# The first up quad of each layer as seven products, begun while T is made; a fifth weight slot

## What is computed

```
x = x + concat(out_a, out_b) @ w_out          # the out tiles
h = rmsnorm(x, g_ffn)
z = dwconv3_centred(h @ w_up)                 # w_up: 1024 x 5632, gate and value halves
x = x + (silu(z_gate) * z_val) @ w_down       # w_down: 2816 x 1024
```

## Time and profile before

| | us |
|---|---|
| runs | 1079.54, 1079.80, 1079.80 |
| median | 1079.80 |
| the profiled execution | 1079.64 |
| its span, first to last instruction | 1077.7 |
| TensorE busy | 1063.8 |
| GpSimd, VectorE, ScalarE busy | 701.4, 596.9, 585.3 |

### The profile page before, as it was taken

The page is one execution under the profiler, slowest core; times in us unless marked ns, Lnnn a source line. Parts: engine busy times, 40 slices in busy tenths (PEclk is TensorE's granted clock), DMA queues, the critical chain, the costliest instruction groups (busy, mean ns, idle before and its releaser), DMA issues.

```text
span 1077.7 us, 18823 instructions
## 1 busy us (share of the span) xinstructions
PE 1063.8 (99%) x6780; PEld 949.1 (88%) x6780; DVE 596.9 (55%) x906; ACT 585.3 (54%) x812; POOL 701.4 (65%) x374
## 2 busy tenths in 40 slices
PE   9999999999999999999999999999999999999997
PEld 7788888798899989998878888888979998899987
DVE  4735765856246730776636359466561776136664
ACT  8835435665366633775548344555653774257641
POOL 5333335896999857995534333558959995699940
PEclk9999999999999999999999999999999999999999
DMA  8332124676798757972522221427759976689502
GB/s 305 99 98 79 59 61 155 162 171 196 184 227 216 203 155 171 210 165 96 177 79 87 79 79 60 156 78 181 188 146 267 209 165 195 165 191 236 153 20 78
DMA packets 48048, 161.75 MB, mean 150 GB/s; under 512 B 5584, under 2 KB 8400, under 8 KB 47952
## 3 DMA queue, kind: packets, MB, share of 16 engines
q1 hardware_dynamic: 35728, 117.51, 34.0%
q0 software_dynamic: 11520, 41.95, 21.5%
q10 hardware_dynamic: 704, 1.07, 0.3%
HBM read 137.44 MB, written 2.10 MB: 129 GB/s over the span
## 4 chain that ended last, share of the span: by engine, by line
PE 84%; DVE 5%; issue 4%; ACT 3%; POOL 2%; DMA 1%; DVEq 0%; ACTq 0%; SPq 0%; POOLq 0%
PE acc L1926 12%; PE acc L1929 12%; PE acc L1928 12%; PE acc L1630 11%; PE acc L1631 11%; PE acc L1632 11%; PE acc L1757 3%; PE acc L1758 3%; PE acc L1759 3%; DVE arena L1482 1%; POOL w_lo L543 1%; DVE arena L1419 1%; PE sides L1727 1%; PE sides L1845 1%; PE sides L1829 1%
## 5 line engine op out<-in xcount | busy, mean ns | idle before, releaser
L543 POOL TENSOR_TENSOR w_lo<-w_raw,w_hi 128x1024 fp32r<-128x1024 f32 x108 | 276.2, 2661 | 84.1 <-ACT w_hi L940 68.2
L553 POOL TENSOR_TENSOR w_lo<-w_raw,w_hi 128x1024 fp32r<-128x1024 f32 x52 | 125.2, 2413 | 202.6 <-ACT w_hi L652 202.6
L1630 PE MATMUL acc<-feat_hi,w_hi 128*128 128x512 f32 (+1 forms) x496 | 190.2, 383 | 2.8 <-POOL w_lo L543 1.8
L1631 PE MATMUL acc<-feat_lo,w_hi 128*128 128x512 f32 (+1 forms) x496 | 189.7, 382 | 0.0
L1632 PE MATMUL acc<-feat_hi,w_lo 128*128 128x512 f32 (+1 forms) x496 | 189.6, 382 | 0.0
L1928 PE MATMUL acc<-xg_lo,w_hi 128*128 128x256 f32 x608 | 172.1, 283 | 0.0
L1929 PE MATMUL acc<-xg_hi,w_lo 128*128 128x256 f32 x608 | 172.1, 283 | 0.0
L1926 PE MATMUL acc<-xg_hi,w_hi 128*128 128x256 f32 x608 | 172.0, 283 | 0.0
L1926 PE MATMUL acc<-t_hi,w_hi 128*128 128x256 f32 x480 | 136.0, 283 | 1.2 <-ACT arena L1005 1.2
L1928 PE MATMUL acc<-t_lo,w_hi 128*128 128x256 f32 x480 | 135.8, 283 | 0.0
L1929 PE MATMUL acc<-t_hi,w_lo 128*128 128x256 f32 x480 | 135.8, 283 | 0.0
(11 more groups left out here) (187 smaller groups left out, 2269.2 us busy)
## 6 DMA issues: line engine op xcount, KB each, us to landing
w_raw<-slabs SPq DMA_DIRECT2D x142, 512.0 KB, 4.4
arena<-slabs SPq DMA_DIRECT2D x32, 512.0 KB, 4.4
mixer_sb<-slabs SPq DMA_DIRECT2D x26, 512.0 KB, 5.8
arena<-slabs POOLq DMA_DIRECT2D x20, 512.0 KB, 6.1
w_raw<-slabs POOLq DMA_DIRECT2D x20, 512.0 KB, 5.9
second_s<-slabs SPq DMA_DIRECT2D x10, 512.0 KB, 5.5
second_s<-arena POOLq DMA_DIRECT2D x10, 512.0 KB, 7.8
mixer_sb<-second_s POOLq DMA_DIRECT2D x10, 512.0 KB, 4.9
```

The source lines that it names most:

```text
L543: pool.tensor_tensor(w_lo[:, w], source, w_hi[:, w].bitcast(F32), ALU.subtract).then_inc(lo_done, count)
L553: pool.tensor_tensor(w_lo[:, w], w_raw[:, w], w_hi[:, w].bitcast(F32), ALU.subtract).then_inc(lo_done, 1)
L1630: pe.matmul(out, wh, ah, start=first, stop=False)
L1631: pe.matmul(out, wh, al, start=False, stop=False)
```

## The change

- The first quad becomes a product quad like the ten others, in an order of its own: A11, A12, S4 (which take tokens as they are), then S1, S2, A22, S3. Its units are 28 to 34.
- S4 of that quad needs A12's raw block again (`a12_again`) and is summed in slot 2's raw buffer (`first_s4`).
- T1 is made where it stays: in the block of the tokens' buffer (`xg12_hi`, `xg12_lo`) that is not used in this part. So `gain_hi` and `gain_lo` write only half of the even tiles, `t_high(k)` and `t_low(k)` each have one operation more (256 columns), and the move at the end of the part is gone.
- The room of T1 in feat2 is a fifth weight slot, for S4 of the last quad of the first part and for the fifth down tile. The first four down tiles then wait for units one product earlier (`unit_before`).
- The loads, sums and conversions of the first quad stand among the out tiles on SyncE, GpSimd and ScalarE.

The diff, cut to what matters for the order:

```diff
+FIRST_ORDER = (A11_, A12_, S4_, S1_, S2_, A22_, S3_)
+LAST_OF_FIRST = unit_of(FIRST_QUADS - 1, S4_)
+FIFTH_SLOT = (LAST_OF_FIRST, DOWN_UNIT[0] + RING)
+def unit_before(unit):
+    if unit == LAST_OF_FIRST:
+        return N_FFN - 1
+    if unit == DOWN_UNIT[0] + RING:
+        return LAST_OF_FIRST
+    if DOWN_UNIT[0] <= unit < DOWN_UNIT[0] + RING:
+        return unit - 2 * RING
+    return unit - (2 * RING if unit == DOWN_UNIT[0] + 2 * RING else RING)
...
 # ScalarE
                 def t_high(k):
+
+                    act.wait_ge(t1_raw_done, L * KP + (k + 1))
+                    act.activation(xg12_hi[:, k, :], t1_raw[:, k * H:(k + 1) * H], ACT.Copy).then_inc(t1_hi_done, 1)
                     act.wait_ge(t_raw_done, L * KP + (k + 1))
...
+                high_a11(0)
                 out_tile(4)
                 t_high(1)
+                high_a12(0)
                 out_tile(5)
                 scale_pair(2)
-                first_high(0)
                 out_tile(6)
-                first_high(1)
+                high_s4(0)
+                t_high(2)
                 out_tile(7)
-                t_high(2)
+                high_s1(0)
                 scale_pair(3)
-                first_high(2)
-                first_high(3)
+                copy(0, A11_, 1, u3_copy)
+                high_s2(0)
+                high_a22(0)
+                t_high(3)
                 root("ffn_spread", stdT_done, L * NSIDE + NSIDE, rstdT[:, :], 1.0 / D, S)
-                t_high(3)
-                act.activation(t1_hi, t1_raw, ACT.Copy).then_inc(t1_hi_done, 1)
-                first_quad()
+                high_s3(0)
+                high_s1(1)
+                copy(0, S1_, 3, p5_copy)
+                copy(0, S2_, 1, u2_copy)
+                high_a11(1)
+                high_a12(1)
+                copy(0, S3_, 1, p1_copy)
...
-                    if d == 0:
-                        for to, of in ((xg12_hi, t1_hi), (xg12_lo, t1_lo)):
-                            act.activation(to, of.rearrange("p (k s) -> p k s", k=KP), ACT.Copy).then_inc(t1_moved, 1)
...
 # VectorE
                 def t_low(k):
+                    t1 = t1_raw[:, k * H:(k + 1) * H]
+                    dve.wait_ge(t1_hi_done, L * KP + (k + 1))
+                    dve.tensor_tensor(xg12_lo[:, k, :], t1, xg12_hi[:, k, :].bitcast(F32),
+                                      ALU.subtract).then_inc(t1_ready, 1)
...
-                    if m in (3, 4):
-                        t_low(m - 3)
-                t_low(2)
+                    if m in (3, 4, 6):
+                        t_low(m // 2 - 1 if m > 3 else 0)
+                first_c11()
+                t_low(3)
                 token_scale(L * 2 + 1)
...
-                first_quad()
+                first_rest()
...
 # TensorE
+                def first_products():
...
+                    tile_added(5)
+                    pe.wait_ge(xg_ready, L * 16 + KT + 7)
+                    product(1, unit_of(0, A11_), b11, True)
+                    pe.wait_ge(xg_ready, L * 16 + KT + 8)
+                    product(0, unit_of(0, A12_), b21, True)
+                    pe.wait_ge(o_gated, L * 4 + 2)
+                    pe.wait_ge(ssq_added, (L * 2 + 2) * KT)
+                    spread("ffn_spread", ssq[:, :])
+                    product(2, unit_of(0, S4_), b22, True)
+                    product(3, unit_of(0, S1_), t1, True, t1_ready, L * KP)
+                    pe.wait_ge(copied, L * QUADS * COPIES + 1)
+                    product(1, unit_of(0, S2_), t2, False, t_ready, L * KP)
+                    pe.wait_ge(c11_added, L * QUADS + 1)
+                    product(0, unit_of(0, A22_), t4, True)
+                    pe.wait_ge(copied, L * QUADS * COPIES + 3)
+                    product(1, unit_of(0, S3_), t3, False)
```

More of the change, by code:

```diff
@@ L64 @@
-NS = SLABS_PARTS + FULL_PARTS * PART_SLABS
-SECOND = RING - 1
-LOADS = [SLABS_QUADS // RING + (FULL_PARTS + 1) * (2 if j == RING - 1 else 1) for j in range(RING)]
+LAST = FULL_PARTS
 PART_QUADS = (range(0, FIRST_QUADS), range(FIRST_QUADS, FIRST_QUADS + KP), range(FIRST_QUADS + KP, QUADS))
 PART_TILES = (FIRST_TILES, KT, KT)
[L69 to L76, removed]
@@ new lines @@
+SKIPPED = 3
+QUAD_UNIT, QUAD_SLAB, DOWN_UNIT, DOWN_SLAB = [], [], [], []
+NU = NS = N_FFN
+for d in range(LAST + 1):
+    for q in PART_QUADS[d]:
+        QUAD_UNIT.append(NU)
+        QUAD_SLAB.append(NS)
+        NU, NS = NU + UNITS, NS + RING
+    NU += SKIPPED if d == 0 else 0
+    DOWN_UNIT.append(NU)
+    DOWN_SLAB.append(NS)
+    NU, NS = NU + KT, NS + KT
+assert N_FFN % RING == 0 and NU % RING == 0 and all(n % RING == 0 for n in DOWN_UNIT)
+PARITY = [1, 0, 1] + [1, 0, 1, 0] * FULL_PARTS
@@ L101, with bank_of, counted @@
+def bank_of(q):
+    return (3, 2) if q % 2 == 0 else (2, 3)
+def counted(n):
+    return 1 + SKIPPED if n == LAST_OF_FIRST else 1
+SECOND = RING - 1
+LOADS = [N_FFN // RING + 2 + FULL_PARTS * (2 if j == RING - 1 else 1) for j in range(RING)]
+COPIES = 4
 HALVES = (slice(0, S // 2), slice(S // 2, S))
@@ new lines, in load_first_part @@
+                load_down(L, 0, 2)
+                low_of(L, unit_of(2, S2_))
+                load_a21(L, 3)
+                low_of(L, unit_of(2, A22_))
+                load_down(L, 0, 3)
+                low_of(L, unit_of(2, S3_))
+                load_a11(L, 3)
+                low_of(L, unit_of(2, S4_))
+                load_s2(L, 3)
+                load_a12(L, 3)
+                for m in range(RING, KT):
+                    low_of(L, DOWN_UNIT[0] + m - RING)
+                    load_down(L, 0, m)
@@ L621, in _ @@
-                low(at + N_FFN, raw(0))
+                low_slabs(at + (RING if L == 0 else 0), at + N_OUT + RING)
+                low(L, N_OUT + 4, raw(0))
+                add_s1(L, 0)
+                low(L, N_OUT + 5, raw(1))
+                combine(L, 0)
+                low(L, N_OUT + 6, raw(2))
+                add_s2(L, 0)
+                low(L, N_OUT + 7, raw(3))
+                combine(L, 1)
+                first_s4(L)
+                low_of_quad(L, 0, A11_)
+                add_s3(L, 0)
@@ L2002, in down_products @@
                             pe.wait_ge(feat_ready, feats + k + 1)
-                        last = three(acc[j][:, :], w_block(j, k * P), feat(k), k == 0, k == blocks - 1)
+                        last = three(acc[j][:, :], weights(n + j, k * P, P), feat(k), k == 0, k == blocks - 1)
                         if k == blocks - 1:
```

546 lines of the change are left out of this document (241 added, 305 removed).

## The result

| | before | changed | forecast |
|---|---|---|---|
| median of the runs, us | 1079.78 | 1095.07 (1094.69 to 1096.63) | 1084.1 (1078.0 to 1088.5) |
| profiled execution: its time, its span | 1079.64, 1077.7 | 1096.63, 1094.8 | |
| ratio to before | 1 | 1.0145, 95% interval 1.0127 to 1.0162 | 1.004 |

The account below looks back on a forecast made before the run. TensorE, busy 99% of the span, bounds the kernel. Layer 0: -4.4 gained, +1.6, +3.9 and +1.0 of new waits make +2.1; layer 1 +2.5; together +4.5 us on 1079.64, so 1084.1 (range 1078.0 to 1088.5).

Parts of the forecast that it names:

- Price of the products: First quad on TensorE: seven products of 24 matmuls at 0.120 us replace four at 0.2265, gaining 1.6 us per layer.
- the waits that go: TensorE waits removed in layer 0: 1.05 us at S1, 0.8 at P1's copy, 1.0 at the fourth down tile.
- The wait for P1's copy: First product quad of the kernel before: a TensorE wait behind a queued copy would go, gaining 0.8 us per layer.
- A12: First quad: TensorE would wait 3.9 us for tile 7's low tokens, due at 198.05 after A11 ended at 194.2.
- always late by that: t_lo before tile 7 would wait for GpSimd's S4 low part, 192.4 to 194.8, and end at 195.65.
- A11: First quad: TensorE would wait 1.6 us for tile 6's low tokens, ending at 191.2 but wanted at 189.7.
- T1's low part at tile 4: VectorE would make it from 182.7 to 183.1, before GpSimd's A12 low part; t_lo would then wait until 185.2.
- S2 of the second quad: TensorE would newly wait 1.0 us there, between 0.3 and 2.2, without S4 covering the chain after S3's copy.
- part of the three stood on this chain: From S3's copy to P1's copy, only some of three earlier VectorE operations of 0.6 us would shorten the 10.5 us.
- The clock: Rival: TensorE's clock falls in the new waits, 2 us lost once per layer, giving 1086 to 1088; chance 0.16.
- rival 2: VectorE is hardly blocked by GpSimd: A12 waits 0.65 us, A11 nothing, time 1074.3, faster; chance 0.13.
- Rival 4: The second quad waits more, or the fifth slot and later loads starve the down tiles: 1088 and above; chance 0.09.

Follow-up runs that it names:

- e3_s4_waits: Changed kernel where GpSimd starts S4's low part only once VectorE has made t_lo of tiles 4 and 5; 1088.84 us.
- e4_copy: Changed kernel where, in the second quad alone, ScalarE copies P1 right behind A22's high part, ahead of two centre taps and a SiLU; 1088.78 us.
- e7_filled_less: Changed kernel with 10, 17 and 9 unread small matmuls filling TensorE's idle time ahead of A11, A12 and the second quad's S2; 1089.37 us.
- e8_before_idle: Kernel before, with TensorE waiting ahead of the first up tile until the squares of all out tiles are added, once per layer; 1087.48 us.
- e9_vector_low: e5_order_copy where VectorE, not GpSimd, makes the low part of S2 of the first quad; 1077.72 us.
- e5_order_copy: Changed kernel with the edits of e2_order and e4_copy together; 1079.67 us.
- e2_order: Changed kernel with VectorE's T conversions of tiles 2 and 3 moved behind tile 5's square, of tiles 4 and 5 behind tile 7's; 1080.91 us.

## Where the prediction was right and where wrong

**Price of the products, and the waits that go.** Right. A product of the first quad takes 2.88 us (24 x 0.120). The waits at S1 and at the fourth down tile are gone. The wait for P1's copy was taken out at 0.8 and put in again at 1.0 as the wait of the second quad: it is one and the same, see below. The down tiles of the first part, from the wait for the features to the next part, take 19.86 us where they took 21.06: a gain of 1.2, where the sum had 1.0.

**A12.** Right: 4.05 us where the sum had 3.9, by the steps as walked. All of them came 0.8 to 0.9 us later than walked, and so did the end of A11, so this lateness stands in A11's wait and not here. The t_lo ahead of tile 7 took 2.43 us ("always late by that"), tile 7 was added at 196.52 (forecast 195.6), and e3_s4_waits shows that the subtraction held it.

**A11.** Mechanism right, size off: 2.45 us where the sum had 1.6. The step that failed is T1's low part at tile 4, "182.7 to 183.1". It was this one that was held, for 3.08 us, and t_lo behind it was then free (0.95). Both of VectorE's operations stood behind the subtraction, not one in front of it, and tile 5 came at 186.72 instead of 186.0; 0.4 of that is the subtraction, which ended at 185.64 and not at 185.2. Two more steps nearly cancel. The low tokens of tile 6 started 4.5 us after tile 5's addition where the walk had 4.1, as it took off all 1.05 us of the high part, though the addition of tile 6 sets their start as soon as 0.5 of it is gone. And they took 0.71 us, not 1.1. VectorE's record begins 0.08 us ahead of GpSimd's (182.86 against 182.94), and it was held all the same: such a race can't be told from starts that lie 0.05 to 0.1 us apart. The Trainium skill (SBUF — State Buffer, "Who interferes with whom") lets the one that issues first go first. With t_lo at 194.16 behind a subtraction of 193.21 and the combine's step at 199.02 behind VectorE's 198.58 the traces agree; at 182.86 the record, taken as the issue, does not.

**S2 of the second quad.** Mechanism right, size off: 2.2 us, the upper bound, where the sum had 1.0. The step that failed is that "part of the three stood on this chain". From S3's copy (220.20) to the end of P1's copy (230.23 + 0.58 = 230.81) are 10.6 us, as long as the 10.5 in the earlier trace rows: that VectorE operations were done earlier did not shorten it. TensorE would have started S2 8.44 us behind the copy (the sum had 8.35). Which link of this chain took up what VectorE gave is not shown; e4_copy shows that ScalarE's order, the copy behind two centre taps and a SiLU, is what TensorE waits for.

**The clock.** This is the term that the sum lacked, and the reason why the time left the range. It was a rival with a chance of 0.16 and a price of 2 us per layer; it came in both layers, twice in each. By the starts of the products it cost 2.7 and 1.5 us in layer 0 and 2.2 and 1.5 in layer 1, 7.9 in all (7.5 by e7_filled_less). Two steps of the rival were too small. It reckoned with one fall per layer of some 4 us at half rate, where there were 6.8 and 3.4 us. And it weighed against itself that "the end of the kernel was already thin in work"; e8_before_idle shows that 3.95 us of standing still between dense stretches is enough. Its reading of the start of the kernel in the earlier trace rows holds: the small matmuls there take 0.21 us up to 5.05 and 0.11 from then on, though the view shows 1.00 for the whole stretch. The Trainium skill (TensorE: Matmul & The Clock Gate, "Why this matters for your kernels") warns of idle gaps between bursts of matmuls. The gaps of 3.95 us (e8_before_idle) and 4.05 us (changed kernel, A12) agree; the falls behind 2.2 us (changed kernel, S2) and 2.44 us (e4_copy and e3_s4_waits, A11) came at gaps shorter than those that it warns of.

**The sum again.** By the profiled executions (1096.63 against the forecast 1084.1, so 12.5): the waits account for 2 x (0.85 + 0.15 + 1.2) = 4.4, the clock for 7.9, the down tiles for -0.4. The last output DMA landed 2.7 us after its issue where it had taken 2.0 in the kernel before, 0.8 more; this does not come with the change, as e9_vector_low has 2.0 and e5_order_copy 2.7. That makes 12.7. By the medians the kernel was 11.0 above the forecast, as the profiled execution of the changed kernel was 1.5 above its own.

**Rivals 1, 2 and 4.** All three lost. VectorE did not keep the lead at tile 4, and the blocking does matter. The condition of rival 2 is nearly what e2_order makes by hand, and there A12 still waits 1.2 us, not 0.65. Rival 4 has its time, above 1088, but not its reason: S2 of the second quad waited no more than the upper bound of the sum, and the down tiles gained 1.2 us.

## What to carry to other kernels

A wait of TensorE is not priced by its length alone: from 2.2 us on, the waits in these runs could bring the half clock for the matmuls behind them, in some kernels and not in others. It cost up to 2.7 us at one place, and nothing where the next product had to wait anyway. When a change lets an engine start earlier, walk the helpers' queues up to the last input of the first products: work for later products put in front of the last tiles (here T of tiles 2 to 5) delays exactly those inputs. Moving it behind them was two numbers in one line and gave 14 of the 15 us back.

## What the runs showed of the hardware

- TensorE's granted clock fell to the 1.2 GHz level at idle stretches of 2.2 to 4 us. It fell while TensorE stood still (0.7 us before A12 in layer 0 of the changed kernel, 1.8 us in layer 1) or after work had begun again (1 us later in e8_before_idle, 1.5 us later behind S2). In mid-kernel it stayed there for 3.4 or 6.8 us each time, though TensorE worked without a break from its next matmul on. None fell at waits of 1.2 to 1.84 us (e2_order).
- From 2.2 to 2.6 us the length of the wait does not decide. Ahead of A11, 2.45 us brought no fall in the changed kernel (both layers), and 2.57 us none in layer 0 of e3_s4_waits; 2.44 us brought one in layer 1 of e3_s4_waits and of e4_copy. Ahead of S2, 2.2 us brought one in the changed kernel and none in e3_s4_waits. What decides there is open.
- At this level a matmul takes 0.213 us for 256 columns and 0.43 for 512, against 0.120 and 0.227.
- A matmul of plain float32 with 128 columns leaves two records and takes 0.223 us (34 records in 3.96 us, e7_filled_less), nearly as long as one of 512 columns of the rounded type that the kernel uses.
- Where VectorE works on two SBUF inputs, one of VectorE and GpSimd waits for the other: a t_lo took 2.43 us behind a GpSimd subtraction and 0.96 once the subtraction came after it (e3_s4_waits), and GpSimd's step of a combine took 1.60 instead of 0.74 behind VectorE's (e9_vector_low).
